# Nine buffers instead of seven for the expert weights of a two-layer diffusion trunk, with one-hots made two experts at a time

## The chip, the cores and the metric

The kernel runs on one core of one Trainium2 chip. The metric is the device time of one execution in microseconds, the median of several runs; lower is better.

## The reference, cut to what matters

256 tokens of width 1024 pass through two layers with attention and feed-forward parts. The last part of the second layer is a mixture of eight experts, of which each token uses two. The change lies in this part:

```python
D_FF_EXPERT = 3584

def moe_swiglu(h, router_w, w1, w3, w2):
    logits = (h @ router_w).astype(jnp.float32)
    top_val, top_idx = lax.top_k(logits, TOP_K)
    gates = jax.nn.softmax(top_val, axis=-1)
    dense_gate = jnp.sum(jax.nn.one_hot(top_idx, N_EXPERTS, dtype=jnp.float32) * gates[..., None], axis=-2).astype(h.dtype)
    out = jnp.zeros_like(h)
    for e in range(N_EXPERTS):
        out = out + dense_gate[..., e:e + 1] * swiglu(h, w1[e], w3[e], w2[e])
    return out
```

Each expert has three matrices of 1024 x 3584 float32, 44 MB; the eight experts read 352 MB from HBM.

## The kernel before

**Slots.** After the router, expert 0 has slot 0 and VectorE ranks the others by their number of tokens, so that slots 0, 2, 4 and 6 ("wide", up to 128 tokens) and slots 1, 3, 5 and 7 ("narrow", up to 64 tokens) alternate. Each slot handles one expert. Tokens of a slot are gathered by a product with a one-hot matrix (`expert_onehot`, `MP`; the program calls it `dispatch`), and its results go back to token order by a product with the transposed one-hot (`expert_onehot_t`, `MPT`; `combine`), which TensorE makes in `turn_onehots` and ScalarE copies out of PSUM (`onehot_turned`). A second round `experts(1)` for overfull experts stands behind a branch and is not executed here.

**Units and the ring.** The weights of a slot arrive in 42 units (`NU`) of 1 MB: 28 of w1 and w3 and 14 of w2. SyncE issues all 336 loads in their order from one queue (`experts(b)` in the sync block, issue line L1209). Load n goes to buffer n mod `NRING` and may start when the unit that used this buffer is free (`raw_free`): in a wide slot when VectorE has made its low part (semaphore `e_low`), in a narrow slot when TensorE has used it (`narrow_used`). There are seven buffers: six of `raw_weights` and the upper half of `y`.

**Wide slots.** ScalarE rounds a unit to a high part (L1543), VectorE subtracts it for the low part (L1829), and TensorE does three products per tile with them (L626, L627, L628), 12 instructions of 512 columns per unit. There are three pairs of buffers for high and low parts (`NSP_E = 3`), so a split waits for TensorE to be done with the unit three before. All four wide slots use the same plane of the gathered-token tiles `xe_high` and `xe_low`, which have two.

**Narrow slots.** TensorE reads the raw units directly (L2492 for w1 and w3, L2509 for w2), eight instructions per unit.

**Between them.** Near the end of a wide slot TensorE gathers the tokens of the next two slots (L2388, `dispatch`) ahead of the last two w2 items. Slot 0 has its tokens gathered before the first unit. In slot 0, behind the first w3 item, TensorE turns the one-hots of all eight slots at once (L2376), and the next item waits until ScalarE has copied the four banks (`mpt_done`).

The overlay is 48 KB per partition that the odd layer's attention used before. In the expert part it held the gathered tokens, the one-hots of eight slots (8 KB), their turns (8 KB), the activations and the results.

Of the kernel before, what the change touches and what calls it, by code (L numbers as in the profile page):

```python
# [20 lines left out]
F32 = mybir.dt.float32  # L21
# [7 lines left out]
P = 128  # L29
# [4 lines left out]
SEQ = 256  # L34
# [18 lines left out]
NRING = NRAW + 1  # L53
# [138 lines left out]
HBANK = (6, 7, 4, 5)  # L192
# [4 lines left out]
def trunk(nc, w, out):  # L197
    ctx = ExitStack()
    with ctx:
# [159 lines left out]
        def plane(e):  # L359

            return (e + 1) % 2

        def gathered(e):

            return (0,) if e < 0 else tuple(i for i in (e + 1, e + 2) if i < NE)

        def tokens_of(b, e):

            return S("xe_low"), NE * 2 * b + 4 * ((e + 1) // 2)

        def gathers_next(e):

            return e % 2 == 0
# [16 lines left out]
        def buffer(b, e, u):  # L390

            i = place(b, e, u) % NRING
            return RAW[:, i, :] if i < NRAW else Y[:, 4:8, :].rearrange("p a n -> p (a n)")

        def raw_full(b, e, u):

            n = place(b, e, u)
            return S(f"eraw{n % NRING}"), 16 * (NU * NE // NRING) * b + 16 * (n // NRING + 1)
# [754 lines left out]
        def _(sp):  # L1153
# [35 lines left out]
            def expert_load(b, e, u):  # L1189
# [12 lines left out]
                else:  # L1202
# [7 lines left out]
                  .then_inc(S(f"eraw{place(b, e, u) % NRING}"), 16)  # L1210

            def experts(b):
                units = sorted(itertools.product(range(NE), range(NU)), key=lambda eu: place(b, *eu))
                named = set()
                for n, (e, u) in enumerate(units):
                    if n >= NRING:
                        sp.wait_ge(*raw_free(b, *units[n - NRING]))
                    elif b == 0 and n >= NRAW:
                        sp.wait_ge(S("htok_full"), 2)
                    elif b == 0:  # L1220
                        sem, v = release[len(UNITS) - NRAW + (u - len(UNITS)) % NRAW]
                        sp.wait_ge(S(sem), v)
                    else:
                        sp.wait_ge(*raw_free(0, NE - 1, NU - NRING + n))
                    if e and e not in named:
                        named.add(e)
                        sp.wait_ge(S("ranked"), 1)
# [34 lines left out]
            sp.wait_ge(S("flag_ready"), 1)  # L1262
# [30 lines left out]
        def _(act):  # L1293
# [189 lines left out]
            for f in range(2):  # L1483
                act.wait_ge(S(f"eraw{f}"), 16)
                act.activation(esplit(f)[0], RAW[:, f, :], ACT.Copy).then_inc(S("e_high"), 1)
# [6 lines left out]
            act.wait_ge(S("top_diff"), 1)  # L1492
# [3 lines left out]
            def experts(b):  # L1496
                def xe_high(e, r):
                    act.wait_ge(S("xe_full"), 20 * b + 4 * ((e + 2) // 2) + r + 1)
                    src = PS[XBANK[r]][:, :].rearrange("p (f e n) -> p f e n", f=2, e=2)
                    for i, s in enumerate(gathered(e)):  # L1500
                        if narrow(b, s):
                            last = act.activation(XEN[:, 2 * r:2 * r + 2, :], src[:, :, i, 0:NARROW], ACT.Copy)
                        else:
                            last = act.activation(XEH[:, plane(s), 2 * r:2 * r + 2, :], src[:, :, i, :], ACT.Copy)
# [23 lines left out]
                def onehot_turned():  # L1528

                    for i in range(4):  # L1530
                        act.wait_ge(S("pt_full"), 4 * b + i + 1)
                        act.activation(MPT[:, 2 * i:2 * i + 2, :], PS[HBANK[i]][:, :].rearrange("p (e n) -> p e n", e=2),
                                       ACT.Copy).then_inc(S("mpt_done"), 1)
# [11 lines left out]
                def narrow_slot(e):  # L1545
                    if e >= 1:
                        ye_high(e - 1)
                    for i, (kind, p) in enumerate(NARROW_ORDER):
# [4 lines left out]
                        if p >= 1:  # L1553
                            gt_whole(e, p - 1)
                    gt_whole(e, NP - 1)
# [12 lines left out]
                for e in range(NE):  # L1568
# [3 lines left out]
                    for i, (kind, j) in enumerate(ORDER):  # L1572
                        for u in (2 * i, 2 * i + 1):
                            if b or u >= (EARLY if e else 2):
                                high_of(e, u)
                            if u == NU - 2 and not gathers_next(e):
# [5 lines left out]
                        if i == 2 and e == 0:  # L1582
                            onehot_turned()
# [6 lines left out]
                        if kind == "d" and j == JE - 2 and gathers_next(e):  # L1590
# [31 lines left out]
        def _(dve):  # L1622
# [230 lines left out]
            dve.tensor_tensor(DIF, MX[:, :, 1], MX[:, :, 0], ALU.subtract).then_inc(S("top_diff"), 1)  # L1853
# [758 lines left out]
```

## Time and profile before

| what | value |
|---|---|
| median of 3 runs | 1845.5 us (1844.99 to 1846.26) |
| the profiled execution, its own time | 1845.54 us |
| its span in the profile | 1843.7 us |
| TensorE busy | 1695.3 us, 92% |
| VectorE busy | 851.7 us, 46% |
| ScalarE busy | 742.4 us, 40% |
| HBM read | 471.25 MB, 256 GB/s over the span |
| mean granted TensorE clock | 0.975 |

The span is what the profiler saw between the first and the last instruction; the profiled execution's own time is 1.8 us longer. The expert part takes the time from about 914 us to the end of the span. Slots begin on TensorE at about 914 (slot 0), 1042 (1), 1146 (2), 1271 (3), 1376 (4), 1502 (5), 1605 (6) and 1731 us (7). A busy share of TensorE near 100% in a wide slot means that its instructions follow each other; the GB/s of a stretch tell whether the weight stream ran.

### The profile page before, as it was taken

The numbers are of one execution on the slowest core, as the hardware profiler recorded it, in microseconds if no ns is written. First come the engines' busy times: TensorE is split into PE (matmuls) and PEld (weight loads), VectorE is DVE, ScalarE is ACT, GpSimd is POOL, SyncE is SP. The second block draws the span as 40 slices with busy tenths as digits, with TensorE's granted clock in tenths as the row PEclk, the third lists the DMA queues.
The fourth block names the chain that finished last, engine by engine and source line by source line (L and its number), as shares of the span: only waits on it lengthen the run. The fifth ranks groups of instructions, "written<-read, shape, count | busy, mean of one in ns | idle before, by whom it ended". The sixth has DMA issues, their size and how long they took to land.

```text
span 1843.7 us, 22005 instructions
## 1 busy us (share of the span) xinstructions
PE 1695.3 (92%) x9050; PEld 1204.0 (65%) x9050; DVE 851.7 (46%) x994; ACT 742.4 (40%) x918; POOL 26.0 (1%) x27
## 2 busy tenths in 40 slices
PE   6998898999999999989999987999879998799986
PEld 4877486888888868757778623886238862388622
DVE  4333736232333354264698501985019850188401
ACT  5332636222223235355567302773027730277301
POOL 0000000000000001030000000000000000000000
PEclk9999998999999999999799999999999999999999
DMA  9644133632223246162789899998999989999896
GB/s 336 204 160 138 43 118 118 205 112 92 92 92 114 92 137 189 30 188 92 258 325 373 331 409 396 394 393 335 409 395 393 374 338 409 396 394 391 338 410 266
DMA packets 238636, 473.82 MB, mean 257 GB/s; under 512 B 16120, under 2 KB 115376, under 8 KB 238528
## 3 DMA queue, kind: packets, MB, share of 16 engines
q1 hardware_dynamic: 238144, 471.38, 70.5%
q8 instruction: 74, 1.21, 0.3%
q0 software_dynamic: 384, 0.95, 0.3%
q14 instruction: 34, 0.28, 0.0%
HBM read 471.25 MB, written 1.05 MB: 256 GB/s over the span
## 4 chain that ended last, share of the span: by engine, by line
PE 74%; DMA 16%; DVE 5%; ACT 3%; issue 1%; SPq 1%; ACTq 0%; DVEq 0%
PE bank L626 19%; PE bank L627 19%; PE bank L628 19%; DMA raw_weights<-in_moe_w 14%; PE bank L2492 5%; PE bank L693 2%; DMA y<-in_moe_w 2%; PE bank L2388 1%; PE bank L483 1%; DMA raw_weights<-in_ev_w_in 1%; PE bank L2427 1%; ACT split_high L605 1%; DVE split_low L1829 1%; SPq L1178 1%; PE bank L701 1%
## 5 line engine op out<-in xcount | busy, mean ns | idle before, releaser
L626 PE MATMUL bank<-h_high,split_high 128*128 128x512 f32 (+1 forms) x832 | 317.2, 381 | 7.5 <-DVE h_low L540 4.1
L627 PE MATMUL bank<-h_low,split_high 128*128 128x512 f32 (+1 forms) x832 | 314.2, 378 | 0.0
L628 PE MATMUL bank<-h_high,split_low 128*128 128x512 f32 (+1 forms) x832 | 314.1, 378 | 0.0
L610 DVE TENSOR_TENSOR split_low<-raw_weights,split_high 128x1024 fp32r<-128x1024 f32 x118 | 144.0, 1225 | 292.3 <-ACT split_high L605 292.3
L1829 DVE TENSOR_TENSOR split_low<-raw_weights,split_high 128x2048 fp32r<-128x2048 f32 x96 | 219.8, 2290 | 75.2 <-ACT split_high L1543 74.5
L1543 ACT ACTIVATE split_high<-raw_weights 128x2048 fp32r<-128x2048 f32 x94 | 180.3, 1918 | 66.8 <-PE bank L628 64.2
L605 ACT ACTIVATE split_high<-raw_weights 128x1024 fp32r<-128x1024 f32 x118 | 124.1, 1056 | 188.4 <-PE bank L628 183.8
L2492 PE MATMUL bank<-raw_weights,xe_narrow 128*64 128x512 f32 (+1 forms) x832 | 170.8, 549 | 22.7 <-DMA raw_weights<-in_moe_w 22.6
L626 PEld LDWEIGHTS bank<-h_high,split_high 128*128 128x128 f32 x832 | 158.6, 191 | 40.8 <-issue 7.9
L628 PEld LDWEIGHTS bank<-h_high,split_low 128*128 128x128 f32 x832 | 158.4, 190 | 28.8
L627 PEld LDWEIGHTS bank<-h_low,split_high 128*128 128x128 f32 x832 | 158.7, 191 | 27.5
L2011 DVE TENSOR_TENSOR residual<-bank,residual 128x512 f32<-128x512 f32 (+1 forms) x44 | 29.1, 662 | 283.9 <-PE bank L2492 283.9
L626 PE MATMUL bank<-split_high,xe_high 128*128 128x512 f32 x336 | 136.7, 407 | 18.0 <-DVE split_low L1829 17.1
L1537 ACT ACTIVATE residual<-bank 128x512 f32<-128x512 f32 (+1 forms) x44 | 25.5, 580 | 317.0 <-PE bank L2492 296.1
L2492 PEld LDWEIGHTS bank<-raw_weights,xe_narrow 128*64 128x64 f32 x832 | 55.8, 136 | 128.3 <-issue 76.8
L627 PE MATMUL bank<-split_low,xe_high 128*128 128x512 f32 x336 | 133.5, 397 | 0.0
L2509 PE MATMUL bank<-raw_weights,gt_narrow 128*64 128x512 f32 x416 | 102.0, 611 | 34.2 <-DMA raw_weights<-in_moe_w 32.3
L628 PE MATMUL bank<-split_high,xe_low 128*128 128x512 f32 x336 | 133.4, 397 | 0.0
L1829 DVE TENSOR_TENSOR h_low<-raw_weights,h_high 128x2048 fp32r<-128x2048 f32 x48 | 110.0, 2292 | 26.2 <-ACT h_high L1543 26.2
L1543 ACT ACTIVATE h_high<-raw_weights 128x2048 fp32r<-128x2048 f32 x48 | 92.1, 1920 | 26.4 <-PE bank L628 23.9
L2509 PEld LDWEIGHTS bank<-raw_weights,gt_narrow 128*64 128x64 f32 x416 | 26.4, 137 | 104.7 <-DMA raw_weights<-in_moe_w 55.3
L626 PEld LDWEIGHTS bank<-split_high,xe_high 128*128 128x128 f32 x336 | 65.0, 193 | 34.2 <-DVE split_low L1829 20.4
(311 smaller groups left out, 2392.3 us busy)
## 6 DMA issues: line engine op xcount, KB each, us to landing
raw_weights<-in_moe_w SPq DMA_DIRECT2D x288, 1024.0 KB, 10.4
raw_weights<-in_w_mod SPq DMA_DIRECT2D x48, 1024.0 KB, 6.6
y<-in_moe_w SPq DMA_DIRECT2D x48, 1024.0 KB, 10.2
raw_weights<-in_ffn_w SPq DMA_DIRECT2D x33, 1024.0 KB, 5.3
raw_weights<-in_ev_w_in SPq DMA_DIRECT2D x10, 1024.0 KB, 10.9
raw_weights<-in_od_w_in SPq DMA_DIRECT2D x8, 1024.0 KB, 7.0
raw_weights<-in_ev_w_out SPq DMA_DIRECT2D x4, 1024.0 KB, 6.4
raw_weights<-in_od_w_out SPq DMA_DIRECT2D x4, 1024.0 KB, 7.9
```

The source lines that it names most:

```text
L605: act.activation(half_of(s, j, SPH[:, s % NSPLIT, :]), half_of(s, j, raw_of(r)), ACT.Copy)\
L610: dve.tensor_tensor(half_of(s, j, SPL[:, s % NSPLIT, :]), half_of(s, j, raw_of(split_at[s])), half_of(s, j, SPH[:, s % NSPLIT, :]).bitcast ...
L626: pe.matmul(ps, wh, xh, start=first, stop=False)
L627: pe.matmul(ps, wh, xl, start=False, stop=False)
L628: return pe.matmul(ps, wl, xh, start=False, stop=last)
L693: last = pe.matmul(PS[bank][32 * j:32 * j + 32, 256 * (i % 2):256 * (i % 2) + 256], SC[:, 4 * h + j, :], wt[:, 4 * h + j, :], start=(h == ...
L1537: act.activation(SIL[:, :, 0:n], PS[bank][:, 0:2 * n].rearrange("p (a n) -> p a n", a=2), ACT.Silu)\
L1543: act.activation(esplit(u)[0], buffer(b, e, u), ACT.Copy).then_inc(S("e_high"), 1)
L1829: dve.tensor_tensor(lo, buffer(b, e, u), hi.bitcast(F32), ALU.subtract).then_inc(S("e_low"), 1)
L2011: dve.tensor_tensor(GE[:, :, 0:n], PS[bank][:, 0:2 * n].rearrange("p (a n) -> p a n", a=2), SIL[:, :, 0:n], ALU.mult).then_inc(S("ge_free" ...
L2492: last = pe.matmul(bank[NARROW * h:NARROW * h + NARROW, 0:n], XEN[:, kk, :], wt[:, k, h, :], start=(kk == 0), stop=(kk == KT - 1))
L2509: last = pe.matmul(PS[4][NARROW * h:NARROW * h + NARROW, :], GTN[:, p % 2, g:g + NARROW], wt[:, k, h, :], start=(p == 0 and f == 0), stop= ...
```

## The change

- The ring has nine buffers: two new ones of 8 KB per partition (`spare_weights`) in the overlay, then the six of `raw_weights`, then the half of `y`. The first two units no longer wait for the last weights of the trunk; the following six take the `raw_weights` buffers in the order in which the trunk frees them.
- The room comes from the overlay: one plane of `xe_high` and `xe_low` instead of two (`xe_narrow` has its own place now), one-hots for two slots instead of eight, their turns for two pairs of slots.
- One-hots are therefore made pair by pair: for slot 0 ahead of its gather, for slots 1 and 2 in slot 0 at item 10 (of 21, numbered from 0; an item is two units), for 3 and 4 in slot 2, for 5 and 6 in slot 4, for 7 in slot 6 (`onehots`, on VectorE).
- They are turned pair by pair too: slot 0's in slot 0 behind the second w3 item, the others' in the narrow slot that opens the pair, behind its second w3 item. Bank 7 alone holds a turn (`HBANK`). The next gather and the combine wait for ScalarE's copy, and the item behind the turn does not.
- Four semaphores of the router are merged into one counter, `routed`, with the same order.

```diff
-NRING = NRAW + 1
+NSPARE = 2
+NRING = NSPARE + NRAW + 1
+GROUPS = NE // 2 + 1
-HBANK = (6, 7, 4, 5)
+HBANK = 7
-        XEN = under("xe_narrow", [P, KT, NARROW])
-        XEH, XEL = sb("xe_high", [P, 2, KT, CAP], F32R), sb("xe_low", [P, 2, KT, CAP], F32R)
+        XEH, XEL = sb("xe_high", [P, KT, CAP], F32R), sb("xe_low", [P, KT, CAP], F32R)
+        XEN = sb("xe_narrow", [P, KT, NARROW])
-        MP = sb("expert_onehot", [P, 2, NE, CAP], F32R)
-        MPT = sb("expert_onehot_t", [P, NE, SEQ], F32R)
+        MP = sb("expert_onehot", [P, 2, 2, CAP], F32R)
+        MPT = sb("expert_onehot_t", [P, 2, 2, SEQ], F32R)
+        SPARE = sb("spare_weights", [P, NSPARE, UNIT])
...
-            i = place(b, e, u) % NRING
-            return RAW[:, i, :] if i < NRAW else Y[:, 4:8, :].rearrange("p a n -> p (a n)")
+            i = (NE * NU * b + place(b, e, u)) % NRING
+            if i < NSPARE:
+                return SPARE[:, i, :]
+            return raw_of(len(UNITS) + i - NSPARE) if i < NRING - 1 else Y[:, 4:8, :].rearrange("p a n -> p (a n)")
...
                     if n >= NRING:
                         sp.wait_ge(*raw_free(b, *units[n - NRING]))
-                    elif b == 0 and n >= NRAW:
+                    elif b == 0 and n < NSPARE:
+                        sp.wait_ge(S("y_evac1"), 1)
+                    elif b == 0 and n < NRING - 1:
+                        sem, v = release[len(UNITS) - NRAW + n - NSPARE]
+                        sp.wait_ge(S(sem), v)
+                    elif b == 0:
                         sp.wait_ge(S("htok_full"), 2)
-                    elif b == 0:
-                        sem, v = release[len(UNITS) - NRAW + (u - len(UNITS)) % NRAW]
-                        sp.wait_ge(S(sem), v)
...
+                def onehots(e, at):
+
+                    g = group(b, e + 1)
+                    if g:
+                        dve.wait_ge(S("pt_full"), g)
+                    for i, s in enumerate(gathered(b, e)):
...
-                for e in range(1, NE):
-                    last = onehot(e, SPOS)
-                last.then_inc(S("onehot"), 1)
...
+                        if i == 10 and gathers_next(b, e):
+                            onehots(e, SPOS)
...
-                def turn_onehots():
-                    for i in range(4):
-                        for e in range(2):
-                            for t in range(2):
-                                last = pe.matmul(PS[HBANK[i]][:, 256 * e + P * t:256 * e + P * t + P],
-                                                 MP[:, t, 2 * i + e, :], IDR[:, :], start=True, stop=True)
-                        last.then_inc(S("pt_full"), 1)
+                def turn_onehots(e):
+                    for i in range(len(gathered(b, e - 1))):
+                        for t in range(2):
+                            last = pe.matmul(PS[HBANK][:, SEQ * i + P * t:SEQ * i + P * t + P], MP[:, t, i, :],
+                                             IDR[:, :], start=True, stop=True)
+                    last.then_inc(S("pt_full"), 1)
...
+                            if p == 1:
+                                turn_onehots(e)
...
-                            if j == 1 and e == 0:
-                                pe.wait_ge(S("mpt_done"), 4 * b + 4)
-                            elif j == 1:
+                            if j == 1 and e >= 1:
                                 pe.wait_ge(S("comb_done"), 4 * (NE * b + e))
...
-                            if j == 0 and e == 0:
-                                pe.wait_ge(S("onehot"), b + 1)
+                            if j == 1 and turns_onehots(b, e):
                                 pe.wait_ge(S("grow"), 2)
-                                turn_onehots()
+                                turn_onehots(e)
```

Lines of the changed file stand 15 to 29 higher in the expert part (L626 is L641 there, L1209 is L1224, L1829 is L1848, L2376 is L2399).

SyncE, the first loads of the expert part, before (`mod_used` is counted by the trunk's last modulation units, `htok_full` by the router's stage, `e_low` by VectorE's splits):

```order
L1178 DMA raw_weights<-in_w_mod 128x8x256 [waits mod_used] x2
L1209 DMA raw_weights<-in_moe_w 128x4x512 [waits mod_used] x6
L1209 DMA y<-in_moe_w 128x4x512 [waits htok_full]
L1209 DMA raw_weights<-in_moe_w 128x4x512 [waits e_low]
L1209 DMA raw_weights<-in_moe_w 128x2x1024 [waits e_low] x2
```

and of the change (`y_evac1` is counted when the attention's output product has its first tile out):

```order
L1193 DMA raw_weights<-in_w_mod 128x8x256 [waits mod_used] x2
L1224 DMA spare_weights<-in_moe_w 128x4x512 [waits y_evac1] x2
L1224 DMA raw_weights<-in_moe_w 128x4x512 [waits mod_used] x6
L1224 DMA y<-in_moe_w 128x2x1024 [waits htok_full]
L1224 DMA spare_weights<-in_moe_w 128x2x1024 [waits e_low]
```

Seven loads stood ahead of the first that waits for a split; now nine do, and every later load stands two frees ahead of where it stood.

TensorE in slot 0, behind the fourth unit, before:

```order
L626 MATMUL bank<-split_high,xe_high 128x512
L627 MATMUL bank<-split_low,xe_high 128x512
L628 MATMUL bank<-split_high,xe_low 128x512
L2376 MATMUL bank<-ident_r,expert_onehot 128x128 [waits grow,onehot]
L2376 MATMUL bank<-ident_r,expert_onehot 128x128 x15
L626 MATMUL bank<-split_high,xe_high 128x512 [waits e_low,mpt_done]
```

and of the change, there and four units further on (behind unit 7):

```order
L643 MATMUL bank<-split_high,xe_low 128x512
L641 MATMUL bank<-split_high,xe_high 128x512 [waits e_low]
...
L643 MATMUL bank<-split_high,xe_low 128x512
L2399 MATMUL bank<-ident_r,expert_onehot 128x128 [waits grow]
L2399 MATMUL bank<-ident_r,expert_onehot 128x128
L641 MATMUL bank<-h_high,gt_high 128x512 [waits e_low,gt_low]
```

The sixteen turns and the wait for `mpt_done` are gone from behind unit 3; two turns stand behind unit 7, and what follows them waits for no copy.

VectorE in slot 0, between the splits of units 3 and 4, before (`angles` is the router's scratch, `expert_onehot` the one-hots of slots 1 to 7):

```order
L1829 TENSOR_TENSOR split_low<-raw_weights,split_high 128x2048 [waits e_high,vector_step]
L1928 TENSOR_SCALAR expert_onehot<-constants,angles 128x128 x2
L1932 TENSOR_SCALAR expert_onehot<-constants,angles 128x128 x2
...
L1928 TENSOR_SCALAR expert_onehot<-constants,angles 128x128 x2
L1903 TENSOR_TENSOR angles<-angles,constants 128x64
L1904 TENSOR_REDUCE angles<-angles 128x8 [waits vector_step]
L1955 CAST angles<-angles 128x8 [waits vector_step]
L1829 TENSOR_TENSOR split_low<-raw_weights,split_high 128x2048 [waits e_high]
```

and of the change, there and at item 10 of the slot (again in slots 2, 4 and 6):

```order
L1848 TENSOR_TENSOR split_low<-raw_weights,split_high 128x2048 [waits e_high,vector_step]
L1922 TENSOR_TENSOR angles<-angles,constants 128x64
L1923 TENSOR_REDUCE angles<-angles 128x8 [waits vector_step]
L1977 CAST angles<-angles 128x8 [waits vector_step]
L1848 TENSOR_TENSOR split_low<-raw_weights,split_high 128x2048 [waits e_high]
...
L1951 TENSOR_SCALAR expert_onehot<-constants,angles 128x128 [waits pt_full]
L1951 TENSOR_SCALAR expert_onehot<-constants,angles 128x128
L1957 TENSOR_SCALAR expert_onehot<-constants,angles 128x128 x2
L2033 TENSOR_TENSOR residual<-bank,residual 128x2x256 [waits gt_full,esilu,e_slots]
```

Fourteen instructions left the place between two early splits; four of them stand ahead of a product (L2033) in the middle of each wide slot.

## Rows read from the trace of the kernel before

**Rows 1.** The page: GB/s over the span in 40 slices of 46.1 us

```profile
GB/s 336 204 160 138 43 118 118 205 112 92 92 92 114 92 137 189 30 188 92 258 325 373 331 409 396 394 393 335 409 395 393 374 338 409 396 394 391 338 410 266
```

**Rows 2.** Busy time by stretch: slots 0, 1, part of 1, 2, 3, 7

```profile
core 0: us, PE busy (x) PEld busy (x) DVE busy (x) ACT busy (x) POOL busy (x), PEclk, DMA share, GB/s
930.00:1040.00 110.00, 108.52 (x508) 90.36 (x507) 96.36 (x72) 76.97 (x57) 0.00 (x0) 1.00 0.98 363
...
1042.00:1145.00 103.00, 82.79 (x391) 27.13 (x390) 8.29 (x11) 8.94 (x13) 0.00 (x0) 1.00 1.00 388
1080.00:1100.00 20.00, 15.61 (x68) 4.25 (x66) 0.00 (x0) 1.18 (x2) 0.00 (x0) 1.00 1.03 409
1145.00:1263.00 118.00, 117.42 (x530) 96.30 (x531) 104.50 (x60) 84.51 (x56) 0.00 (x0) 0.99 1.04 392
...
1271.00:1375.00 104.00, 83.75 (x390) 27.37 (x386) 8.13 (x11) 8.57 (x13) 0.00 (x0) 0.98 1.00 389
...
1731.00:1830.00 99.00, 82.51 (x390) 26.97 (x386) 6.52 (x10) 5.45 (x11) 0.00 (x0) 1.00 0.95 372
```

**Rows 3.** Chain that ended last, slot 3 to the start of slot 4

```profile
1270.78 7.02 PE bank L2492 x32
...
1288.61 11.43 DMA raw_weights<-in_moe_w
...
1300.08 1.96 PE bank L2492 x8
...
1302.19 17.28 DMA raw_weights<-in_moe_w
...
1371.45 1.92 ACT split_high L1543
1373.39 2.30 DVE split_low L1829
...
1375.73 0.80 PE bank L626
```

**Rows 4.** SyncE's loads in order of time, around slot 2 to 3

```profile
1262.70 0.37 SPq L1209 DMA_DIRECT2D y<-in_moe_w  x1
1272.69 2.22 SPq L1209 DMA_DIRECT2D raw_weights<-in_moe_w  x2
```

**Rows 5.** Busy time by stretch, where the four narrow slots begin

```profile
1038.00:1046.00 8.00, 8.00 (x38) 4.46 (x39) 1.29 (x2) 1.09 (x2) 0.00 (x0) 1.00 0.35 121
...
1268.00:1276.00 8.00, 8.00 (x39) 3.83 (x39) 1.29 (x2) 1.09 (x2) 0.00 (x0) 1.00 0.30 88
...
1498.00:1506.00 8.00, 8.00 (x38) 4.37 (x38) 1.29 (x2) 1.09 (x2) 0.00 (x0) 1.00 0.39 127
...
1728.00:1736.00 8.00, 8.00 (x39) 3.83 (x39) 1.29 (x2) 1.09 (x2) 0.00 (x0) 1.00 0.36 115
```

**Rows 6.** Chain that ended last, slot 0 behind unit 3

```profile
926.96 0.41 PE bank L2376 x4
...
927.38 1.36 ACT expert_onehot_t L1532 x3
...
929.57 0.47 PE bank L626
```

**Rows 7.** VectorE in order of time, between the splits of units 3 and 4

```profile
923.80 0.48 DVE L1928 TENSOR_SCALAR expert_onehot<-constants,angles 128x128 fp32r<-128x128 f32 x2
...
926.54 0.22 DVE L1903 TENSOR_TENSOR angles<-angles,constants 128x64 f32<-128x64 f32 x1
...
927.13 2.29 DVE L1829 TENSOR_TENSOR split_low<-raw_weights,split_high 128x2048 fp32r<-128x2048 f32 x1
```

**Rows 8.** SyncE's and ScalarE's first expert instructions, in order of time

```profile
891.29 7.67 SPq L1209 DMA_DIRECT2D raw_weights<-in_moe_w  x6
...
896.65 1.89 ACT L1485 ACTIVATE split_high<-raw_weights 128x2048 fp32r<-128x2048 f32 x1
```

**Rows 9.** Busy time by stretch, the first 10 us of slot 4

```profile
1375.00:1385.00 10.00, 9.27 (x30) 6.79 (x32) 7.22 (x4) 6.10 (x5) 0.00 (x0) 0.72 1.05 387
```

More of the change, by code:

```diff
@@ L357, in blocks_before, with gathers_next, gathered, group @@
             return JE * wide_before(b, e) + NP * (e // 2 if b == 0 else NE // 2)
[L359 to L365, printed above, removed]
+        def gathers_next(b, e):
+            return e + 1 < NE if b else e % 2 == 0
+        def gathered(b, e):
+            if b or e < 0:
+                return (e + 1,)
+            return tuple(i for i in (e + 1, e + 2) if i < NE)
+        def group(b, e):
+            return GROUPS + e if b else (e + 1) // 2
+        def item(b, e):
+            return 1 if b == 0 and e and e % 2 == 0 else 0
+        def turns_onehots(b, e):
+            return b == 1 or e == 0 or e % 2 == 1
         def tokens_of(b, e):
-            return S("xe_low"), NE * 2 * b + 4 * ((e + 1) // 2)
-        def gathers_next(e):
-            return e % 2 == 0
+            return S("xe_low"), 4 * (NE // 2 + e if b else group(b, e))
         def raw_free(b, e, u):
@@ L1575, in experts @@
                                 high_of(e, u)
-                            if u == NU - 2 and not gathers_next(e):
+                            if u == NU - 2 and not gathers_next(b, e):
                                 gt_high(e, JE - 1)
@@ L1936, in experts @@
-                onehot(0, POS if b == 0 else SPOS).then_inc(S("onehot_first"), 1)
+                def onehots(e, at):
+                    g = group(b, e + 1)
+                    if g:
+                        dve.wait_ge(S("pt_full"), g)
+                    for i, s in enumerate(gathered(b, e)):
+                        for t in range(2):
+                            if narrow(b, s):
+                                last = dve.tensor_scalar(MP[:, t, i, :].rearrange("p (o n) -> p o n", o=2),
+                                                         CON[:, C_IOTA:C_IOTA + NARROW]
+                                                         .rearrange("p (o n) -> p o n", o=1)
+                                                         .to_broadcast([P, 2, NARROW]), at[:, t, s:s + 1], None,
+                                                         ALU.is_equal)
+                            else:
+                                last = dve.tensor_scalar(MP[:, t, i, :], CON[:, C_IOTA:C_IOTA + P], at[:, t, s:s + 1],
+                                                         None, ALU.is_equal)
+                    last.then_inc(S("onehot"), 1)
@@ L2036, in experts @@
                                 next_low(e, u)
-                            if u == NU - 2 and not gathers_next(e):
+                            if u == NU - 2 and not gathers_next(b, e):
                                 gt_low(e, JE - 1)
@@ L2411, in up @@
                             kk = 4 * q + k
-                            last = three(pe, bank[:, :], XEH[:, plane(e), kk, :], XEL[:, plane(e), kk, :], hi[:, a],
+                            last = three(pe, bank[:, :], XEH[:, kk, :], XEL[:, kk, :], hi[:, a],
                                          lo[:, a], kk == 0, kk == KT - 1)
```

92 lines of the change are left out of this document (45 added, 47 removed).

## The prediction, made before the changed kernel ran

> **What bounds the kernel now.** I read the page's slices first, then the busy time by stretch for each slot of the expert part, then the chain that ended last, then SyncE's loads. The expert part fills the second half of the span. In the slices its weight stream has a pattern: 409, 396, 394, 391 and then a slice of 335 to 338, once per pair of a wide and a narrow slot [rows 1]. That dip is what I wanted explained.
>
> By slots [rows 2]: in wide slot 2 TensorE is busy 117.4 of 118 us while the stream runs at 392 GB/s. In narrow slots 1 and 3 TensorE is busy only 83 of 103 to 104 us. The chain says what it waits for [rows 3]: from 1270.8 us it runs on the units that lie ready, from 1288.6 us on nearly all time is put down to transfers, with single units of work (1.96 us) between them, until the first unit of slot 4 has been rounded (1.92), subtracted (2.30) and multiplied from 1375.7 us on. In steady narrow work, the stretch from 1080, the stream gives 409 GB/s [rows 2], that is 1.0486 MB / 409 = 2.56 us for a unit that TensorE uses in 1.96 us. So a narrow slot is bound by the stream, a wide slot by TensorE, and the time of a pair is: wide slot, plus the time in which the stream brings what the ring did not hold when the wide slot ended.
>
> At that border the stream stands still. SyncE issues a load at 1262.7 us, for the buffer that the last split of slot 2 freed, and the next at 1272.7 us, when the first narrow unit has been used [rows 4]. Between those TensorE gathers tokens and finishes w2 from split copies; no raw buffer comes free. In the 8 us around this the stream moves 88 GB/s of its 409, and 121, 127 and 115 at the other three borders [rows 5]. Lost time is 8 x (1 - rate/409): 5.6, 6.3, 5.5 and 5.8 us. The ring is full, and its depth of seven is what ends the stream.
>
> **The ring of nine, the large term.** With two more buffers every load may be issued two frees earlier. At each of the four borders from wide to narrow two more units are loaded or under way, and the narrow slot has two fewer to wait for. Two units are 2 x 2.56 = 5.13 us. Each border has at least 5.5 us of standstill, so the stream can take them all: 4 x 5.13 = 20.5 us. In slot 2, where the stream ran without pause at 392 GB/s up to the end, the lead comes from the standstill itself: the loads issued by 1262.7 us carry the stream to about 1268.5, two more to 1273.6, and the next is issued at 1272.7. At the first border it comes otherwise: slot 0 starts with nine units instead of seven, and its stream (363 GB/s, below what the same loads reach in slot 2 [rows 2]) has room to keep the lead.
>
> Does the slot behind give it back? A wide slot starts when its first unit has landed and takes its 118 us of TensorE work from there; it moves earlier as a whole. In the narrow slots TensorE must fit its work into less: 83 us of work (slot 3, 83.8) in about 99 us, slot 7 82.5 in about 94 [rows 2]. There is cover of over 10 us, so TensorE doesn't become the bound. Slot 7 is last, and its gain goes straight into the end. The least I can give per border is half, if the split of a wide slot's last units is delayed and the lead isn't reached: 2.6 us. The most is the whole standstill, 5.8 on average.
>
> The Trainium skill prices a transfer otherwise: "DMA: Bandwidth & Descriptors", section on the anatomy of one DMA, has a fixed part of about 2 us and then 436 GB/s. By that, as an estimate, a megabyte costs 2.4 us of stream, two 4.8, and four borders 19.2 us instead of 20.5. This trace shows 409 in steady flow [rows 2], and the fixed part only where the stream had stood; I stay with the row.
>
> **Turns and one-hots in slot 0, the small term.** Behind unit 3 TensorE makes sixteen turns from 926.96 us, waits for ScalarE's copies, and starts unit 4 at 929.57 [rows 6]. Both are gone there. What is next in line is VectorE's split of unit 4, which begins at 927.13 behind fourteen one-hots (923.80 to 926.54, 0.2 us each) [rows 7]. Without them it begins at 923.80 + 0.59 (the three short steps from 926.54 to 927.13) = 924.4 and ends at 926.7, as TensorE arrives; the rounding by ScalarE was done before. So unit 4 starts at about 927.0, 2.6 us earlier. Two turns four units later cost at most half of the first four's 0.41 us [rows 6]. Net 2.4 us. Slot 0 is bound by TensorE (108.5 of 110 us busy [rows 2]), so its end, and the restart of the stream, move by it. Bounds: 0, if the split of unit 4 or 5 is late by another wait, and 3.
>
> **What is added.** The fourteen one-hots move to the middle of wide slots: 4, 4, 4 and 2, about 0.8 us each time ahead of a product. VectorE is busy 104.5 of 118 us in slot 2 [rows 2]. What covers them: a split buffer that comes free is needed again two units later, 24 instructions of 0.23 us or 5.5 us; rounding and subtracting take 1.92 + 2.30 = 4.2 us [rows 3], which leaves 1.3 us for a delay of 0.8. I take zero; with no cover it is 14 x 0.2 = 2.8 us. The four turns in narrow slots 1, 3 and 5 (below 0.5 us each) and ScalarE's copies lie in the 20 us in which TensorE waits for the stream; zero, at most 1.4 us together. The new wait on `mpt_done` at the next gather stands a whole slot behind its copy.
>
> The first loads are issued earlier than 891.29 us, two at once and six as the trunk's last units are used. Nobody gains: ScalarE rounds the first unit at 896.65 with no wait before it [rows 8]. Nobody behind these loads is held either, since they are the next in the queue anyway. Zero; if the earlier stream disturbed the router's stage I would see it there, and no row prices it.
>
> **Sum.** 1845.54 (the profiled execution's own time, its span of 1843.7 and 1.8 around it) - 20.5 - 2.4 = 1822.6 us. The median of the runs shown is 1845.5, practically the same.
>
> **The rivals.**
> - *Half the lead.* The two extra units are filled late, because a wide slot loads hardly faster than TensorE uses: from 1145 to 1263 us at 392 GB/s the stream moves 44.1 units' worth in 118 us against 42 used [rows 2]. If later wide slots eat the lead, each border gives about 2.6 us: 10.3 + 2.4, so 1833 us. Against it: SyncE stands waiting for a buffer at each border [rows 4, 5], which needs a full ring. 10%.
> - *The ring gives nothing.* Both slot kinds run at the rate of the stream with standstills that are needed anyway; only the 2.4 us stay: 1843 us, within 0.2% of before. The stretch at 88 GB/s between two at about 400 speaks against it. 5%.
> - *Slower: more transfers in flight make the stream slower.* Up to nine 1 MB transfers can be outstanding instead of seven. The narrow slots load 168 units at 2.56 us; the gain of 22.9 us is eaten when a unit costs 0.136 us more, at 388 GB/s. At the 372 of slot 7's whole stretch [rows 2], which has its standstill in it, a unit takes 2.82 us, 168 x 0.26 = 43 us more, 1866 us. Against it: 409 GB/s come in a stretch in which the ring is drained and all seven are outstanding, more than the 392 of a wide slot, where units lie landed in the ring. 5%.
> - *The clock.* Each wide slot starts with TensorE at half its 2.4 GHz for some microseconds, after the wait for the first split; in slot 4 the granted mean of 10 us is 0.72 [rows 9], which is 2.8 us lost of those 10; over slot 2's 118 us it is 0.99 [rows 2], 1.2 us. Three slots can draw either way: 3 to 4 us. This widens the range on both sides and has no chance of its own.
>
> **How the numbers follow.** A change of 0.2%, 3.7 us, is about what a measurement of this kernel can tell from none. My forecast, 1822.6 us, has 80% for its mechanism; its own range is 1818.5 (standstill fully taken, 4 x 5.8 = 23.2 in place of 20.5, and a good draw of the clock) to 1827 (2.8 for the one-hots, or a bad draw). The half lead has 10%, the two others 5% each. The range for 8 in 10 reaches from 1818 to 1831, halfway and more into the half lead. Faster by over 0.2%: 80 + 10, less 1 for a sum of small misses, 0.89; within 0.2%: 0.06; slower: 0.05.
>
> **What would show it.** In the profile of the changed kernel: at the borders to slots 3, 5 and 7 no stretch of 8 us under 300 GB/s, and at the border to slot 1 one that is still low, with SyncE's wait as long as before; narrow slots of 98 to 99 us instead of 103 to 104, with TensorE's work unchanged; slot 7 of about 94. In slot 0 TensorE goes from unit 3 to unit 4 without a gap and the slot ends 2.4 us earlier. VectorE busy in a wide slot 0.8 us more, TensorE still over 99%. The prediction is wrong if the GB/s in narrow slots fall below 400, if the borders keep their standstill, or if TensorE shows gaps behind the one-hots in the middle of a wide slot.

## The result, and the profile after

The changed kernel takes 1823.0 us (median of 4 runs, 1820.7 to 1825.0) against 1845.2 (1844.2 to 1846.3): a ratio of 0.988, 95% interval [0.986, 0.990]. That is 22.2 us less; 1822.6 was forecast. On another chip it gave 1824.6 and 0.988 [0.986, 0.990] again. The profiled execution took 1822.02 us, its span is 1820.1.

The slices of the page of the changed kernel, in the form of [rows 1]:

```profile
GB/s 336 195 178 139 29 134 116 208 93 101 108 93 93 93 113 240 0 200 90 290 299 368 327 409 399 393 394 374 411 397 394 393 370 410 396 394 394 370 409 262
```

The dip once per pair is 370 to 374 now; it was 335 to 338. Busy time by stretch of the changed kernel, cut at its own borders (slots 0 to 4 and 7), as [rows 2]:

```profile
923.50:1030.00 106.50, 105.04 (x481) 86.60 (x480) 96.78 (x72) 76.03 (x52) 0.00 (x0) 1.00 0.98 362
1038.30:1136.50 98.20, 81.95 (x395) 28.02 (x394) 8.80 (x11) 9.90 (x14) 0.00 (x0) 1.00 0.99 386
1136.50:1254.00 117.50, 117.46 (x527) 95.95 (x528) 104.25 (x62) 84.15 (x56) 0.00 (x0) 0.99 1.04 396
1262.20:1360.80 98.60, 81.97 (x395) 27.89 (x395) 8.81 (x11) 10.10 (x14) 0.00 (x0) 0.99 1.00 389
1360.80:1479.00 118.20, 118.20 (x528) 96.54 (x529) 104.39 (x63) 83.95 (x56) 0.00 (x0) 0.98 1.04 397
...
1712.00:1806.00 94.00, 81.72 (x392) 27.60 (x390) 6.51 (x10) 5.71 (x11) 0.00 (x0) 1.00 0.95 371
```

Narrow slots last 98 to 99 us from their first unit to TensorE's first product of the next slot, 103 to 105 before, with about the same TensorE work in them (82 us). Wide slots are as long as they were within 1 us. The chain that ended last of the changed kernel, slot 3 to the start of slot 4 (compare [rows 3]):

```profile
1262.19 7.02 PE bank L2520 x32
...
1271.24 13.88 PE bank L2520 x64
...
1285.71 7.02 PE bank L2520 x32
...
1303.51 19.00 DMA raw_weights<-in_moe_w
...
1356.50 1.92 ACT split_high L1560
1358.44 2.30 DVE split_low L1848
```

TensorE runs on what lies ready until about 1300 us, 38 us into the slot; it was 18 us before. I use two marks of this view for every kernel below: the first narrow unit and the first low part of the next wide slot. Between them lie 96.25 us here and 102.61 in [rows 3].

The border itself, by SyncE's loads and by stretch (the first two rows are loads, the others 8 us of the four borders), of the changed kernel:

```profile
1254.24 0.37 SPq L1224 DMA_DIRECT2D y<-in_moe_w  x1
1264.23 2.12 SPq L1224 DMA_DIRECT2D spare_weights<-in_moe_w  x2
...
1034.00:1042.00 8.00, 8.00 (x38) 4.59 (x38) 1.29 (x2) 1.08 (x2) 0.00 (x0) 1.00 0.38 130
...
1260.00:1268.00 8.00, 8.00 (x38) 3.56 (x38) 1.29 (x2) 1.09 (x2) 0.00 (x0) 1.00 0.70 257
...
1485.00:1493.00 8.00, 8.00 (x38) 3.42 (x38) 1.29 (x2) 1.08 (x2) 0.00 (x0) 1.00 0.62 222
...
1709.00:1717.00 8.00, 8.00 (x37) 3.84 (x37) 1.29 (x2) 1.09 (x2) 0.00 (x0) 1.00 0.60 205
```

SyncE waits 10 us as before. The standstill, by 8 x (1 - rate/409) as in the prediction, is 5.5, 3.0, 3.7 and 4.0 us. It is not gone, and yet each narrow slot is 4.5 to 6.4 us shorter. The experiments say why.

### The profile page after: what moved, and what is told of

It is laid out like the page before. It is cut to its first block, busy times and chain, and to the rows that moved or that the text cites. A ratio compares the mean times of both kernels' runs of the same rounds, so it can differ in the third digit from the quotient of the medians.

```text
span 1820.1 us, 22016 instructions
## 1 busy us (share of the span) xinstructions
PE 1688.8 (93%) x9050; PEld 1205.1 (66%) x9050; DVE 850.9 (47%) x994; ACT 742.7 (41%) x919; POOL 26.0 (1%) x27
## 3 DMA queue, kind: packets, MB, share of 16 engines
HBM read 471.25 MB, written 1.05 MB: 259 GB/s over the span
## 4 chain that ended last, share of the span: by engine, by line
PE 77%; DMA 11%; DVE 5%; SPq 3%; ACT 3%; issue 1%; DVEq 0%; ACTq 0%
PE bank L641 20%; PE bank L643 19%; PE bank L642 19%; PE bank L2520 6%; DMA raw_weights<-in_moe_w 6%; SPq L1224 2%; DMA spare_weights<-in_moe_w 2%; PE bank L708 2%; DMA y<-in_moe_w 2%; PE bank L2537 1%; PE bank L2415 1%; PE bank L2453 1%; PE bank L498 1%; PE bank L716 1%; DMA raw_weights<-in_w_mod 1%
## 5 line engine op out<-in xcount | busy, mean ns | idle before, releaser
L641 PE MATMUL bank<-h_high,split_high 128*128 128x512 f32 (+1 forms) x832 | 317.8, 382 | 6.7 <-DVE h_low L555 4.0
L625 DVE TENSOR_TENSOR split_low<-raw_weights,split_high 128x1024 fp32r<-128x1024 f32 x118 | 144.0, 1225 | 292.7 <-ACT split_high L620 292.7
L1848 DVE TENSOR_TENSOR split_low<-raw_weights,split_high 128x2048 fp32r<-128x2048 f32 x74 | 169.3, 2289 | 50.0 <-ACT split_high L1560 49.5
L641 PEld LDWEIGHTS bank<-h_high,split_high 128*128 128x128 f32 x832 | 159.0, 191 | 39.7 <-issue 7.8
L1560 ACT ACTIVATE split_high<-raw_weights 128x2048 fp32r<-128x2048 f32 x74 | 141.9, 1918 | 53.8 <-PE bank L643 51.9
L2520 PE MATMUL bank<-raw_weights,xe_narrow 128*64 128x512 f32 (+1 forms) x696 | 138.6, 539 | 16.9 <-DMA raw_weights<-in_moe_w 16.6
L641 PE MATMUL bank<-split_high,xe_high 128*128 128x512 f32 x336 | 137.1, 408 | 17.1 <-DVE split_low L1848 17.1
L2033 DVE TENSOR_TENSOR residual<-bank,residual 128x512 f32<-128x512 f32 (+1 forms) x44 | 29.1, 662 | 263.3 <-PE bank L2520 263.3
L2520 PEld LDWEIGHTS bank<-raw_weights,xe_narrow 128*64 128x64 f32 x696 | 47.2, 136 | 101.4 <-issue 64.4
L1848 DVE TENSOR_TENSOR split_low<-spare_weights,split_high 128x2048 fp32r<-128x2048 f32 x38 | 87.0, 2289 | 26.5 <-ACT split_high L1560 25.9
L1848 DVE TENSOR_TENSOR h_low<-raw_weights,h_high 128x2048 fp32r<-128x2048 f32 x38 | 87.1, 2291 | 20.1 <-ACT h_high L1560 20.1
L641 PEld LDWEIGHTS bank<-split_high,xe_high 128*128 128x128 f32 x336 | 65.0, 194 | 34.3 <-DVE split_low L1848 20.6
L1560 ACT ACTIVATE h_high<-raw_weights 128x2048 fp32r<-128x2048 f32 x38 | 72.9, 1919 | 20.1 <-PE bank L643 18.5
L2537 PE MATMUL bank<-raw_weights,gt_narrow 128*64 128x512 f32 x288 | 67.9, 601 | 13.9 <-DMA raw_weights<-in_moe_w 13.0
```

Source lines behind the costliest of these rows:

```text
L625: dve.tensor_tensor(half_of(s, j, SPL[:, s % NSPLIT, :]), half_of(s, j, raw_of(split_at[s])), half_of(s, j, SPH[:, s % NSPLIT, :]).bitcast ...
L641: pe.matmul(ps, wh, xh, start=first, stop=False)
L1560: act.activation(esplit(u)[0], buffer(b, e, u), ACT.Copy).then_inc(S("e_high"), 1)
L1848: dve.tensor_tensor(lo, buffer(b, e, u), hi.bitcast(F32), ALU.subtract).then_inc(S("e_low"), 1)
L2033: dve.tensor_tensor(GE[:, :, 0:n], PS[bank][:, 0:2 * n].rearrange("p (a n) -> p a n", a=2), SIL[:, :, 0:n], ALU.mult).then_inc(S("ge_free" ...
L2520: last = pe.matmul(bank[NARROW * h:NARROW * h + NARROW, 0:n], XEN[:, kk, :], wt[:, k, h, :], start=(kk == 0), stop=(kk == KT - 1))
```

## The experiments

All start from the changed kernel. Slot lengths are between the marks above. For narrow slots 1, 3, 5 and 7 (the last to ScalarE's final copy) before gave 101.15, 102.61, 101.23 and 98.99 us, 404.0 in all; the changed kernel 95.86, 96.25, 96.74 and 94.24, 383.1. Slot 0 is taken from the first row of its gather to the first narrow unit: 134.9 and 132.6 us.

### A ring of seven, and of eight

```diff
-NSPARE = 2
+NSPARE = 0
```

(and `NSPARE = 1`; the memory of the buffers stays reserved.)

> The changed kernel with NSPARE = 0, so a ring of seven again (the one-hots and turns stay pair by pair). Theory 'depth': only slot 0's 2.4 us remain of the gain, and the time returns to 1823.0 + 4 x 5.13 = 1843.5 us (1841 to 1846); narrow slots take 103 to 104 us, and the 8 us around their starts carry 90 to 130 GB/s. Rival 'regrouping': the gain came from taking the one-hots, turns and the wait out of the early slot and from the second plane's room; then it stays within 4 us of 1823.

> The changed kernel with NSPARE = 1, a ring of eight. Theory 'depth': half of the way, 1823.0 + 4 x 2.56 = 1833.3 us (1831.5 to 1835.5), narrow slots of 101 us. Rival 'the first buffer does nearly all' (any standstill is gone once one more transfer is in flight): within 3 us of 1823. Rival 'only the pair helps' (a split or a load pattern that needs two): within 3 us of ring7's time.

Measured: 1844.5 us with seven (0.9998 of before, [0.9986, 1.001]) and 1835.4 with eight (0.996, [0.994, 0.997]). The chain of the ring of seven, and under it that of the ring of eight, at slot 3:

```profile
1271.59 7.02 PE bank L2520 x32
...
1373.61 2.30 DVE split_low L1848
```

```profile
1268.60 7.02 PE bank L2520 x32
...
1367.47 2.30 DVE split_low L1848
```

102.0 and 98.9 us, then 96.25 with nine. Over the four narrow slots: 404.4, 392.8, 383.1. The eighth buffer takes 11.7 us off, the ninth 9.7; two units of 2.56 us at four borders were to be 20.5, and 21.3 came. "Depth" holds, in steps of about one transfer per buffer and border, and the rivals fall. The medians are rougher: steps of 9.1 and 12.4 us. In the profiled executions eight and nine buffers are 12.8 us apart, and 2.4 of them lie ahead of slot 0's gather, where a kernel's executions differ anyway (the changed kernel itself begins it at 905.7 us in one profile and at 909.1 in another). At the border to slot 3 the ring of eight looks as before:

```profile
1266.00:1274.00 8.00, 8.00 (x38) 3.75 (x38) 1.29 (x2) 1.08 (x2) 0.00 (x0) 1.00 0.29 86
```

Its standstill is as long as with seven (6.3 us in [rows 5]), and the slot is 3.7 us shorter than in [rows 3]. So the gain doesn't have to come out of the standstill. The wide slots show where it comes from. Slot 4 with seven, eight and nine buffers, between the marks, and for each the 30 us up to 6 us ahead of the second mark:

```profile
1373.61:1501.37 127.76, 125.42 (x574) 102.77 (x576) 108.96 (x68) 87.70 (x63) 0.00 (x0) 0.99 1.01 381
1465.40:1495.40 30.00, 30.00 (x152) 25.49 (x151) 26.31 (x17) 21.27 (x19) 0.00 (x0) 1.00 1.00 373
```

```profile
1367.47:1495.31 127.84, 125.50 (x574) 102.89 (x576) 108.98 (x68) 87.68 (x63) 0.00 (x0) 0.99 1.02 390
1459.30:1489.30 30.00, 30.00 (x151) 25.49 (x150) 26.36 (x17) 21.26 (x19) 0.00 (x0) 1.00 1.03 407
```

```profile
1358.44:1487.06 128.62, 126.27 (x574) 103.38 (x576) 108.97 (x68) 87.69 (x63) 0.00 (x0) 0.97 1.04 396
1451.00:1481.00 30.00, 30.00 (x151) 25.46 (x151) 26.36 (x17) 21.26 (x19) 0.00 (x0) 1.00 1.03 407
```

Time by rate, in units of 1.0486 MB, gives 46.4, 47.5 and 48.6 units brought by the time the narrow slot begins: one more per buffer. A ring of seven is full before the wide slot ends and holds the stream to 373 GB/s there; with eight it runs at 407, and 34 GB/s more over 30 us are one unit. The ninth buffer changes nothing there, and its unit comes at the border.

### The gather ahead of the last but one item

```diff
                         elif j < JE - 1:
+                            if j == JE - 2 and gathers_next(b, e):
+                                for r in range(3):
+                                    dispatch(e, r)
...
-                                dispatch(e, 0)
-                                dispatch(e, 1)
                                 turn(e, JE - 1)
-                                dispatch(e, 2)
                                 dispatch(e, 3)
```

(and the copies of ScalarE and VectorE in the same order.)

> The changed kernel with three of the four parts of the gather for the next two slots placed ahead of the last but one w2 item instead of behind it (2.9 us of TensorE work moved away from between the last split of a wide slot and the first narrow unit). My prediction counted the standstill of the stream as lost time; theory 'standstill' then gives up to 2.9 us at each of four borders back, 1823.0 - 11 = 1812 us. Theory 'capacity': the ring is full when the narrow slot begins whatever the standstill's length, and the narrow slot's length is only what the ring doesn't hold by then; so the standstill shrinks in the trace but the narrow slots keep 96 us up to the first split, and the time stays at 1823 within 2.

In the kernel before and the changed one the gather stands ahead of the last w2 item only, which is two units. Measured: 1828.0 us (0.991, [0.989, 0.993]), slower than the changed kernel and outside the time of both theories. SyncE's loads at the border to slot 3:

```profile
1259.88 0.37 SPq L1224 DMA_DIRECT2D y<-in_moe_w  x1
1268.13 2.12 SPq L1224 DMA_DIRECT2D spare_weights<-in_moe_w  x2
```

This wait is 8.3 us instead of 10.0, and the narrow slots take 96.6, 96.2, 96.6 and 94.4 us, within 0.8 us of those without this edit. But the standstill of the stream, which both theories took for shorter, is not. The 40 us that begin 26 us ahead of slot 3, of the changed kernel and then of this one:

```profile
1236.20:1276.20 40.00, 40.00 (x198) 27.33 (x198) 22.29 (x20) 16.43 (x20) 0.00 (x0) 1.00 0.96 370
```

```profile
1240.10:1280.10 40.00, 39.11 (x193) 26.34 (x193) 21.07 (x19) 15.23 (x20) 0.00 (x0) 1.00 0.92 356
```

The stream moves less here, and over all four borders it loses 23 us by the same formula where the changed kernel loses 20 (in 26 us around each narrow slot's start). What SyncE no longer waits for behind the last split it waits for ahead of it: its waits for splits from 1225 to 1270 us are 16.3 us instead of 12.4 (12.3 in the changed kernel's other profile, whose border lies as late as here). So the edit moved the standstill and did not shorten it, and it can't decide between the theories. It agrees with "capacity" in that slot lengths don't follow SyncE's last wait; the rings of seven and eight are what shows the capacity. What the edit costs is a wait of TensorE that the changed kernel doesn't have. TensorE's waits from 1230 to 1270 us, the end of slot 2 (us in total, times, longest):

```profile
PE bank L641 <- DVE gt_low L2026: 0.9, 1, 0.9
```

and TensorE's busy time in 8 us at the ends of slots 4 and 6, where the changed kernel has 8.00:

```profile
1485.00:1493.00 8.00, 7.41 (x32) 5.06 (x34) 1.89 (x4) 1.37 (x4) 0.00 (x0) 1.00 0.76 306
1709.00:1717.00 8.00, 7.01 (x35) 5.32 (x36) 1.69 (x2) 1.28 (x3) 0.00 (x0) 1.00 0.92 367
```

By this kernel's order three of the gather's copies stand on VectorE ahead of the last item, whose low part (`gt_low`) TensorE now waits for: 0.9 us in slot 2 and, by its waits there, in slot 0, and idle times of 0.6 in slot 4 and 1.0 in slot 6. That is 3.4 us of the 3 to 5 us to the changed kernel.

### Late first loads

```diff
-                    elif b == 0 and n < NSPARE:
-                        sp.wait_ge(S("y_evac1"), 1)
-                    elif b == 0 and n < NRING - 1:
-                        sem, v = release[len(UNITS) - NRAW + n - NSPARE]
+                    elif b == 0 and n < NRING - 1:
+                        sem, v = release[len(UNITS) - 1]
```

> The changed kernel, but its first eight loads all wait for the trunk's last weight unit, as the seven of before did (nine buffers stay). My prediction held that the earlier loads are worth nothing: 1823.0 us within 1. Rival 'the early loads fill the ring ahead of slot 0': up to 2 x 2.56 = 5 us slower at the first narrow slot, 1828 us, with slots 2, 4 and 6 unchanged in length.

Measured: 1825.2 us (0.990, [0.989, 0.992]), 2.2 us above the changed kernel where 1 was allowed. SyncE issues the first at 892.6 us instead of 878.2. Slot 0 takes 132.6 and slot 1 96.3 us, as in the changed kernel: the ring is full in time. The gather begins 3.5 us later than in the changed kernel's profile (909.2 against 905.7), but 909.1 is also what the changed kernel itself gave on another chip. The rival, up to 5 us at the first narrow slot, falls. The early loads are worth nothing that I can show; 1825.2 against 1823.0 and 1824.6 is within what chips and runs differ.

### The fourteen one-hots back between two splits

```diff
                 if b == 0:
+                    for k in range(14):
+                        dve.tensor_scalar((YEH, YEL)[k // 8][:, P * (k % 8):P * (k % 8) + P],
+                                          CON[:, C_IOTA:C_IOTA + P], SPOS[:, k % 2, 1:2], None, ALU.is_equal)
                     picked(NUMBER, iota8)
```

> The changed kernel with 14 further one-hots of 128 columns on VectorE at the old place, between the splits of units 3 and 4 of slot 0 (written to free tiles, used by nobody); turns and the wait stay away. Theory 'VectorE's split was next': TensorE gets unit 4 at about 2.4 to 2.6 us later again, all of slot 0's gain is gone and the time is 1823.0 + 2.4 = 1825.4 us. Rival 'the turns and ScalarE's copies were the cost': the extra one-hots are hidden, TensorE goes on from unit 3 to unit 4 within 0.5 us, and the time stays at 1823.

Measured: 1828.6 us (0.991, [0.990, 0.993]). The chain in slot 0, where TensorE gets unit 4:

```profile
923.59 1.57 DVE ye_high L1977 x8
925.16 1.17 DVE ye_low L1977 x6
...
926.84 2.30 DVE split_low L1848
...
929.18 0.50 PE bank L641
...
930.51 0.43 PE bank L642
```

The time was forecast as 1825.4. TensorE waits 2.5 us in the trace, as forecast, so VectorE's split was next in line, and taking only the turns and their wait away would have gained nothing. But slot 0 lengthens by 4.3 us, not 2.4. The rows show it: from 930.5 us a product takes 0.43 us in place of 0.23, and the granted clock of 926 to 936 us is 0.83 where the changed kernel has 1.00. The idle 2.5 us brought a stretch at 1.2 GHz, 1.7 us more. In the kernel of before the wait was in the same place, but TensorE made turns in most of it and idled 0.9 us [rows 6]; there the products kept their 0.23 us and the clock its 1.00.

### More one-hots in the middle of wide slots

```diff
                         if i == 10 and gathers_next(b, e):
+                            for k in range(8 if b == 0 else 0):
+                                dve.tensor_scalar(YEL[:, P * k:P * k + P], CON[:, C_IOTA:C_IOTA + P],
+                                                  SPOS[:, k % 2, 1:2], None, ALU.is_equal)
                             onehots(e, SPOS)
```

> The changed kernel with eight further one-hots (1.6 us of VectorE) at item 10 of each wide slot, ahead of the pair's own, written to a free tile and used by nobody. Theory 'a cover of 1.3 us': 2.4 us of delay against 1.3 leaves about 1.1 us of gap on TensorE in slots 0, 2 and 4 and 0.7 in slot 6, 1823.0 + 4 = 1827 us, with a wait on VectorE's split in the middle of each wide slot. Rival 'VectorE has 13 us free per wide slot and hides it all': 1823. Rival 'nothing is hidden, the pair's own one-hots cost too': + 6.4 us, 1829.4.

Measured: 1831.2 us (0.993, [0.991, 0.995]). TensorE's waits in slot 2, of the changed kernel and then of this one:

```profile
PE bank L641 <- DVE split_low L1848: 5.0, 1, 5.0
```

```profile
PE bank L641 <- DVE split_low L1848: 6.5, 2, 5.0
```

1.5 us more in slot 2, 1.4 in slots 0 and 4, 1.1 in slot 6, 5.4 in all; 4 was forecast. 2.4 us of delay leave a gap of 1.5, so the cover is 0.9 to 1.0 us, thinner than the 1.3 I had worked out, and the pair's own 0.8 us just fits under it: the changed kernel's only wait is the 5.0 us at the start of the slot. VectorE's 13 idle us per slot are no cover for a block in one place. By its time, 1829.4 us, the rival "nothing is hidden" is the nearest; the trace of the changed kernel, which has no wait in mid-slot, speaks against its second half. These gaps leave 1 to 3 us to the changed kernel's medians unexplained; in the profiled executions, 9.9 us apart, 2.6 lie ahead of slot 0's gather, which the edit doesn't touch, and 1.4 in the narrow slots.

### The wide slot's first units early

```diff
-EARLY = 0
+EARLY = 2
```

(and `EARLY = 1`; the constant exists in both kernels at 0.)

> The changed kernel with EARLY = 2: the first two units of the next wide slot are loaded and split ahead of the narrow slot's last two, so that TensorE doesn't wait for the first split. Theory: TensorE starts the wide slot within 0.5 us of where it did, since two more units must land first (5.1 us against the 4.2 us of rounding and subtracting), but it comes without the gap of 5 us, and the half clock (3.4 to 6.8 us of it at three wide slots) is gone: 2 to 3 us for each of slots 2, 4 and 6, 1823 - 6 = 1817 us (1813 to 1821). Rival 'the gap isn't what lowers the clock', or the order costs what it brings: 1823 or above.

Measured: 1823.2 us (0.989, [0.987, 0.991]). The wait of 5.0 us for the wide slot's first split is gone from the trace, and yet the time is the same and the half clock is still there. So I ran it again, beside the changed kernel and a version with one unit:

> The changed kernel once more, on the chip of the two runs that follow. Theory: 0.988 of before, within its interval [0.986, 0.990]; slots 1, 3, 5 and 7 again 94 to 97 us. If the ratio moved by more than 0.002, the differences of 2 to 5 us between the other kernels would be those of the chips and not of the edits.

> EARLY = 2 once more, beside the changed kernel. Theory 'only the gap went': its trace lost the 5 us wait of TensorE at slots 2, 4 and 6 but kept the half clock, and from slot 1 to the end it was 1.6 us shorter; so 0 to 3 us faster than the changed kernel. Rival: it is a draw of the clock, and the two are the same within 1 us.

> EARLY = 1: one unit of the next wide slot ahead of the narrow slot's last. Theory: TensorE has unit 0 ready when it ends the narrow slot, one megabyte (2.56 us) later than the first wide unit landed, starts 2.2 us earlier than with EARLY = 0 but waits 2 us for unit 1; the same as the changed kernel within 2 us. Rival: the shorter gap keeps the clock, 3 to 6 us faster.

Measured on one chip: 1824.6 (changed kernel, 0.988), 1821.6 (two units, 0.987, [0.985, 0.989]) and 1820.1 us (one unit, 0.987, [0.985, 0.988]). Four runs each: 1820.9 to 1826.4, 1820.2 to 1823.1, 1818.7 to 1822.8. One unit early is the fastest that I have, by 4.6 us in the medians; the intervals of the ratios overlap, so this is likely and not proven. The traces set aside what lies ahead of slot 1. From the first narrow unit to the end of the span the changed kernel takes 781.8 us in both its profiles, two units early 780.4 and 781.4, one unit early 778.1: 3.7 us for one unit, and about 1 for two, where the rival of a mere draw is as near as the gain. TensorE's waits over 1 us around the border from slot 1 to slot 2, of the changed kernel, of two units early and of one:

```profile
PE bank L641 <- DVE split_low L1848: 5.0, 1, 5.0
```

```profile
PE bank L2537 <- DMA raw_weights<-in_moe_w: 5.8, 1, 5.8
```

```profile
PE bank L2537 <- DMA raw_weights<-in_moe_w: 3.1, 1, 3.1
PE bank L641 <- DVE split_low L1848: 1.3, 1, 1.3
```

So the premise of the expectations for two units, "without the gap of 5 us", was wrong. Two wide units taken ahead of the last two narrow ones are two transfers that these come later, and TensorE waits 5.8 us for them instead. With one unit early the idle time comes in two pieces, here of 3.1 and 1.3 us, at slot 4 of 3.1 and 2.1, at slot 6 of 3.1 and 0.9. Twenty microseconds around the start of slot 4, with all the idle time in them, of the changed kernel on that chip and then with one unit early:

```profile
1359.00:1379.00 20.00, 15.07 (x55) 11.09 (x56) 14.11 (x10) 12.49 (x8) 0.00 (x0) 0.83 1.05 390
```

```profile
1354.00:1374.00 20.00, 14.82 (x63) 9.04 (x60) 12.90 (x9) 11.90 (x8) 0.00 (x0) 1.00 1.05 389
```

The full clock is kept here, with as much idle time. At slots 2 and 6 the same stretch has 0.91 with one unit early. The changed kernel on that chip has 0.83 at all three; but in the profile of the result slot 2 has 0.91 too, with the same wait of 5.0 us:

```profile
1131.00:1151.00 20.00, 15.00 (x59) 10.64 (x56) 14.20 (x10) 12.56 (x8) 0.00 (x0) 0.91 1.05 388
```

So what the clock loses at a border is in part a draw, and only the 1.00 at slot 4 is something that no trace with the wait in one piece has. The rival of this expectation, the clock, is the nearer one, with 3.7 to 4.6 us of its 3 to 6; that the shorter pieces keep the clock is likely from three borders and not shown.

## Why the prediction was right, and where it was off

**Likeliest time and sum.** 22.9 us were forecast and 22.2 measured. By terms, in the profiled executions, whose spans are 23.6 us apart: the narrow slots give 20.9 us (20.5 forecast), slot 0 gives 2.3 (2.4). The wide slots 2, 4 and 6 are 1.0 us longer in all, 384.7 against 383.7; the part ahead of the gather happened to be 1.5 us shorter, which is luck, since the changed kernel's own profiles differ by 3.4 us there.

**The large term** is shown by the rings of seven and eight. Its size, one transfer per buffer and border, was right within 1 us over all four. Its picture of the border was not. "No stretch of 8 us under 300 GB/s" fails at three borders (257, 222, 205), and the prediction's own sign of being wrong, "if the borders keep their standstill", is met by half: 3.0, 3.7 and 4.0 us are left of 6.3, 5.5 and 5.8. I had both extra units still under way when the last wide split was done. In fact part of the lead is built earlier: the stream in slot 4 runs at 397 GB/s, where the kernel before had 382:

```profile
1375.00:1494.00 119.00, 118.27 (x529) 96.86 (x530) 104.55 (x60) 84.69 (x56) 0.00 (x0) 0.98 1.02 382
```

(slot 2 went from 392 to 396). As an estimate, 15 GB/s more over 118 us are 15 x 118 / 1048.6 = 1.7 units of 1.05 MB in slot 4, and 4 GB/s are 0.45 in slot 2; the rest comes out of the standstill. The count of what the ring holds when the narrow slot starts is what matters, as the prediction's own first part had it ("the time in which the stream brings what the ring did not hold"): each buffer added one unit to it, whether inside the wide slot or at the border. The sum used the standstill only as an upper bound, so nothing broke. The prediction's aside on 2 us and 436 GB/s takes figures that its section gives for transfers issued by the gpsimd path, while these loads go out on SyncE's queue; the sum didn't use them, and the steps of 11.7 and 9.7 us over four borders don't tell 2.4 from 2.56 us a unit.

**The small term** was right in size and in its cause: without the fourteen one-hots and the turns, TensorE goes from unit 3 to unit 4 without a gap, and the one-hots alone bring the gap back. What I hadn't seen is that such a gap can cost the clock on top. By this term the ring of seven should be 2.3 us (0.12%) faster than before. Its slot 0 has them in the trace, 132.5 us against 134.9, but its ratio is 0.9998 ± 0.0012 and doesn't tell 0.12% from nothing. That the term shows in the time by itself stays open.

**The parts costed at nothing.** The one-hots in wide slots are hidden, with 0.1 to 0.2 us to spare and not 0.5. The turns in narrow slots are hidden within 0.4 us (the four narrow slots take 404.4 us with a ring of seven, 404.0 before), and no cost or gain of the early first loads shows.

**The rivals.** Half the lead, no gain and a slower stream all fall: steady narrow work still runs at 409 to 410 GB/s with nine buffers. The clock stayed a matter of width: the same kernel spans 1820.7 to 1826.4 us over two chips.

## What to carry to other kernels

Where slots bound by the engine and slots bound by the stream alternate, a buffer is worth about one transfer time at each border at which the ring is full, as long as the stream can bring one more unit by then, inside the engine-bound slot or in its standstill. A standstill that is as long as before doesn't mean that the buffer brought nothing. Count how much the ring holds when the stream-bound part begins. When a stall is removed, name the next in line on its own engine; and when work is moved into an engine's loop, compare it with the slack between one buffer coming free and its next use, here 1 us, not with the engine's idle time per slot, here 13.

## What the runs showed of the hardware

A gap of TensorE of 2.5 us in slot 0 was followed by products at 0.43 instead of 0.23 us and cost 4.3 us in place of 2.5; a gap of 0.9 us in the same place had not been, and neither were the gaps of 1.5 us in the middle of slots 0 and 2 with more one-hots (granted clock 1.00 in the 20 us around them). At the border to a wide slot, where TensorE has waited for the stream behind every unit before, idle time in one piece of 5.0 us (before, and the kernels with its order) or 5.8 us (two units early) always lowered the clock, but not always by as much: over the 20 us around the slot's start its mean is 0.83 at 22 of the 33 borders traced and 0.91 at 11. With the pieces of one unit early it is 0.91, 1.00 and 0.91. The 1.00 has pieces of 3.1 and 2.1 us, the largest sum of the three, so the sum alone doesn't decide it.

The stream's full rate went with the size of its packets. In the changed kernel it is 387 GB/s from 1136 to 1146 us (1945 packets, 3.87 MB, so 2.0 KB each: a wide slot's w1 and w3 lie in rows of 512 numbers) and 410 from 1070 to 1090 us (2127 packets, 8.19 MB, 3.9 KB each: rows of 1024). So the 397 GB/s of a whole wide slot are a stream that hardly pauses.
